# Split steps moved among gates in the mixer and among rotations, divisions and query copies in the attention of a two-block fp32 network

## What is computed

```python
def short_conv_mixer(h, w_in, conv_w, w_out):
    bcx = h @ w_in
    b_gate, c_gate, u = jnp.split(bcx, 3, axis=-1)
    y = b_gate * causal_depthwise_conv3(c_gate * u, conv_w)
    return y @ w_out

def swiglu(h, w_gate_up, w_down):
    g, u = jnp.split(h @ w_gate_up, 2, axis=-1)
    return (jax.nn.silu(g) * u) @ w_down
...
            kv = rmsnorm(h, kv_norm) @ w_kv
            k_sh = partial_rotary(k_sh.reshape(bsz, s, N_KV_HEADS, HEAD_DIM), cos, sin)
            q = (rmsnorm(h, b_pre_norm[j]) @ b_w_q[j]).reshape(bsz, s, N_HEADS, HEAD_DIM)
            q = partial_rotary(q, cos, sin)
            attn = sliding_window_sink_attention(q, k_sh, v_sh, b_sinks[j]) @ b_w_o[j]
            h = h + rmsnorm(attn, b_post_norm[j])
        ff = swiglu(rmsnorm(h, ffn_pre_norm[l]), ffn_w_gate_up[l], ffn_w_down[l])
```

## Time and profile before

| | |
|---|---|
| median of three runs | 1064.49 us (1064.3 to 1064.68) |
| profiled execution, its own time | 1063.95 us |
| its span, first to last instruction | 1062.1 us |
| TensorE busy | 1049.4 us, 99% |
| VectorE busy | 659.7 us, 62% |
| ScalarE busy | 567.0 us, 53% |
| GpSimd busy | 80.9 us, 8% |
| DMA, mean | 177 GB/s |
| granted TensorE clock, mean | 0.999 |

### The profile page before, as it was taken

How to read it: one execution, slowest core, us unless ns; L and a number is a source line. 1 busy time by engine, 2 the same in 40 slices (tenths; PEclk the granted TensorE clock), 3 DMA queues, 4 the chain that set the end, 5 groups by cost and what they waited for, 6 DMA issues and landing times.

```text
span 1062.1 us, 14789 instructions
## 1 busy us (share of the span) xinstructions
PE 1049.4 (99%) x5023; PEld 861.0 (81%) x5023; DVE 659.7 (62%) x956; ACT 567.0 (53%) x917; POOL 80.9 (8%) x170
## 2 busy tenths in 40 slices
PE   9999999999999999999999999999999999999997
PEld 6998888888877788888888888888887688888886
DVE  5867754546687875554667455456777675555544
ACT  5755644545677664444555444454566744443542
POOL 0034000000023040000001000000101110000001
PEclk9999999999999999999999999999999999999999
DMA  8573656556553354645565465656552253646541
GB/s 341 189 240 124 216 168 211 172 183 201 194 193 105 120 187 163 221 159 200 191 203 180 159 216 162 215 177 212 185 159 80 97 181 120 216 161 216 165 152 40
DMA packets 51883, 187.80 MB, mean 177 GB/s; under 512 B 5808, under 2 KB 5952, under 8 KB 51840
## 3 DMA queue, kind: packets, MB, share of 16 engines
q1 hardware_dynamic: 50688, 183.79, 51.6%
q0 software_dynamic: 864, 3.07, 1.0%
q10 hardware_dynamic: 288, 0.37, 0.1%
HBM read 186.15 MB, written 1.05 MB: 176 GB/s over the span
## 4 chain that ended last, share of the span: by engine, by line
PE 93%; DVE 4%; ACT 2%; issue 1%; POOL 0%; POOLq 0%; DVEq 0%; ACTq 0%
PE pG L1655 17%; PE pG L1653 17%; PE pG L1654 17%; PE pD L1653 11%; PE pD L1655 11%; PE pD L1654 11%; PE pT L1658 3%; DVE w_low L1323 2%; PE pG L1675 1%; PE pG L1658 1%; PE pG L1911 1%; PE pT L1796 1%; ACT w_high L1041 0%; PE pD L1658 0%; PE pD L1930 0%
## 5 line engine op out<-in xcount | busy, mean ns | idle before, releaser
L1323 DVE TENSOR_TENSOR w_low<-raw,w_high 128x1024 fp32r<-128x1024 f32 x340 | 411.2, 1225 | 118.6 <-ACT w_high L1041 104.7
L1041 ACT ACTIVATE w_high<-raw 128x1024 fp32r<-128x1024 f32 x340 | 353.2, 1055 | 79.1 <-PE pG L1655 65.7
L1653 PE MATMUL pG<-w_high,xTh 128*128 128x512 f32 (+1 forms) x816 | 319.8, 392 | 0.1
L1655 PE MATMUL pG<-w_high,xTl 128*128 128x512 f32 (+1 forms) x816 | 312.4, 383 | 0.0
L1654 PE MATMUL pG<-w_low,xTh 128*128 128x512 f32 (+1 forms) x816 | 312.1, 382 | 0.0
L1655 PEld LDWEIGHTS pG<-w_high,xTl 128*128 128x128 f32 x816 | 153.2, 188 | 27.9
L1654 PEld LDWEIGHTS pG<-w_low,xTh 128*128 128x128 f32 x816 | 153.6, 188 | 25.6
L1653 PEld LDWEIGHTS pG<-w_high,xTh 128*128 128x128 f32 x816 | 153.3, 188 | 25.6 <-DVE xTl L1356 0.3
L1653 PE MATMUL pD<-w_high,aTh 128*128 128x512 f32 x384 | 150.8, 393 | 0.0
L1655 PE MATMUL pD<-w_high,aTl 128*128 128x512 f32 x384 | 149.9, 390 | 0.0
L1654 PE MATMUL pD<-w_low,aTh 128*128 128x512 f32 x384 | 149.4, 389 | 0.0
(11 more groups left out here) (266 smaller groups left out, 808.6 us busy)
## 6 DMA issues: line engine op xcount, KB each, us to landing
raw<-in_stream SPq DMA_DIRECT2D x340, 512.0 KB, 4.4
post<-in_posts POOLq DMA_DIRECT2D x5, 512.0 KB, 4.7
early<-in_stream SPq DMA_DIRECT2D x4, 512.0 KB, 12.5
first_w<-in_stream SPq DMA_DIRECT2D x3, 512.0 KB, 6.0
h<-in_x SPq DMA_DIRECT2D x2, 512.0 KB, 5.5
out<-hg SPq DMA_DIRECT2D x3, 256.0 KB, 2.2
consts<-in_consts POOLq DMA_DIRECT2D x1, 417.0 KB, 4.2
out<-hg ACTq DMA_DIRECT2D x1, 256.0 KB, 2.7
```

The costliest lines, as they stand in the source:

```text
L1041: sc.activation(w_high[:, slot(static):slot(static) + CHUNK], raw_of(static), ACT.Copy).then_inc(w_high_done, 1)
L1323: ve.tensor_tensor(w_low[:, slot(static):slot(static) + CHUNK], raw_of(static), w_high[:, slot(static):slot(static) + CHUNK].bitcast(F32), ...
L1653: pe.matmul(dst, ah, hi, start=start, stop=False)
L1655: return pe.matmul(dst, al, hi, start=False, stop=stop)
```

## The change

No operation is added or removed; TensorE, GpSimd and SP have the same instructions in the same order. The change moves splits (and once a rotation) on ScalarE and VectorE:

- start of the mixer: the split of chunk 2 goes ahead of `T(0, 0)`;
- the split of chunk 13 goes from in front of `G(0, 3)` to behind it;
- in `walk_follower`, for blocks 2 to 6 of the mixer, `G(1, b)` goes ahead of the one split that stood in front of it, so that with the two splits that followed it three now stand in a row behind the gate (two for block 6);
- attention: `second(1)` goes ahead of `rope(0, 0)`; one split goes from behind `S(1)` to behind `N(1)`; the two splits around `QKT(0, 1)` go behind `proj(2, 1, 3)` and behind `S(3)`.

```diff
@@ walk_block_step
     if ph.mixer and s == 1:
         step("G", 1, 0, shift)
+    if ph.mixer and s == 3:
+        refill(step, freed, 1)
@@ walk_second_follower
-    refill(step, freed, 2)
+    refill(step, freed, 1)
@@ walk_follower
-    step("R", g, early, shift)
-    step("G", 1, b, shift)
+    if ph.mixer:
+        step("G", 1, b, shift)
+        step("R", g, early, shift)
+    else:
+        step("R", g, early, shift)
+        step("G", 1, b, shift)
@@ walk_attention
+    step("second", 1)
     step("rope", 0, 0)
     projects(0, 1, range(3))
-    step("second", 1)
...
     step("S", 1)
-    refill(step, freed, 1)
     step("E", 1)
...
     step("N", 1)
+    refill(step, freed, 1)
...
     step("N", 2)
-    refill(step, freed, 1)
     step("QKT", 0, 1)
     project(2, 1, 3)
+    refill(step, freed, 1)
     step("rope", 1, 1)
-    refill(step, freed, 1)
     step("PT", 2, 0)
     step("PT", 2, 1)
     step("S", 3)
+    refill(step, freed, 1)
@@ walk
     step("fill", 1, 1)
+    step("fill", 2, 1)
     step("T", 0, 0, 0, ph=MIX)
     step("first", 1, KT // 2, KT)
-    step("fill", 2, 1)
```

## The result

The changed kernel takes 1067.09 us (median of 11 runs, 1066.27 to 1069.32), the kernel before beside it 1064.72 us (11 runs, 1064.05 to 1065.82). The ratio is 1.0025, with a 95% interval of 1.0017 to 1.0032. So the change costs 2.4 us by the medians and 2.7 by the ratio, just beyond the 0.2% (2.1 us) that the prediction took as the border to slower; the interval reaches to both sides of that border. Forecast were +2.0 us and 1066.5. The median lies inside the stated range of 1064.9 to 1067.7, and 0.1 us above the 1067.0 up to which the prediction's own sum was to hold.

What follows compares the result with a forecast made beforehand. TensorE, busy 99% of the span, was taken as the bound, so only its pauses could change. Mixer -0.5 + 2.3 + 1.1 = +2.9, attention -0.95, sum +2.0 us on 1064.49: 1066.5 us, range 1064.9 to 1067.7.

Steps and rivals of the forecast that it cites:

- the prediction's own sum: Whole kernel: mixer +2.9 and attention -0.95 make +2.0 us, 1066.5 us; own range 1065.9 to 1067.0, chance 0.45.
- The removed pauses: Mixer, `T(0, 3)` and `T(1, 2)`: waits vanish, gaining 0.69 and 0.35 us, with 0.05 per transpose pair, together 1.1.
- `T(0, 4)`: Mixer: part of the gain given back through chunk 18's load, leaving 0.5 us gained for all up to here.
- `T(0, 5)`, `T(0, 6)`, `T(0, 7)`: Mixer: new waits for `act` of 0.60, 0.67 and 0.90 us, with 0.05 each, together 2.3 us lost.
- The working by margins: `T(0, 5)` to `T(0, 7)`: each pause is 1.14 us added, less idle time and the margin from `act` to `T`.
- End of the mixer: Block 6: two splits behind the gate delay the taps and TensorE turning `h` by 1.14 us, at least 1.0.
- Attention: -0.95 us: 0.45 at `proj(1, 1, 0)`, 0.5 at `PT(1)`, 0 at `S(3)` because the wait moves to `PV(2)`.
- (a): Rival, mixer: new splits stay hidden, its 1.1 and attention's 0.95 gains kept, no loss at its end; 1062.4 us, chance 0.10.
- (c): Rival, attention: `S(3)` pays after all because `prT` moves up, 0.86 us less, 1065.6 us; chance 0.10.
- (b): Rival, mixer: GpSimd makes splits dearer, last two pauses and mixer end lose 0.2 to 0.3 more each; 1067.2 us, chance 0.35.
- the case that had a chance of 0.43: Verdict on the whole kernel: slower than before by over 0.2% (2.1 us), border 1066.6 us.
- the case beside it: Verdict on the whole kernel: same, within 0.2% (2.1 us) of the kernel before; chance 0.51.

Runs made afterwards that it cites:

- short loads: Changed kernel with the loads of chunks 16 to 19 cut to half their bytes, so part computes on stale weights; one execution, 1066.05 us.
- the split put back: Changed kernel with only the split of chunk 13 back in its old place next to that of chunk 12; 1066.62 us, ratio 1.0023.
- the mixer part alone: Kernel before plus the change's mixer moves and the split ahead of `T(0, 0)`, attention as before; 1068.04 us, ratio 1.0036.
- the kernel with the swap in one follower: Changed kernel, but the gate goes ahead of the split only for follower block 2, not blocks 3 to 6; 1064.14 us, ratio 0.9996.
- the attention part with the split ahead of `E(2)`: Kernel before plus the change's attention moves, with the split behind `project(2, 1, 3)` moved ahead of `E(2)`; 1063.14 us, ratio 0.9985.
- the two attention kernels: Kernel before plus the attention part alone, 1062.79 us (ratio 0.9986), and the same with a split moved ahead of `E(2)`, 1063.14 us (0.9985).
- the kernel that moved the split of block 6: Kernel before, mixer splits two behind gate and two behind leader's `T`, block 6's split behind `D(1, 6)`, attention moves, one split ahead of `E(2)`; 1063.12 us, ratio 0.9988.

## Why the prediction came out as it did

**The removed pauses** were 0.77 and 0.42 us, forecast 1.1 together: right, by the distance between starts and not by the brackets of 0.53 and 0.19.

**`T(0, 4)` is the step that failed.** The prediction says: "The load and everything behind it come 0.5 us earlier, not 1.1." The issue of that load, of chunk 18, did come 0.6 us earlier, but the load landed 0.3 us later, and the splits, `act` and `T(0, 4)` came 0.3 us later with it. The forecast followed this one load, because the row in the trace of before names the wait for it, and took its time to landing as fixed; it was 4.4 us instead of 3.5. What was missed is the load in front of it. SP waits for the moved split of chunk 13 before it issues the load of chunk 17: 43.39 instead of 42.35. The prediction used the moved split to time the split of chunk 14, and did not ask for the load that hangs on it directly. It lands at 48.34, when ScalarE has been idle for 0.62 us, and until then the load of chunk 18 is under way beside it.

The row of four splits was missed at this block too. It costs its 0.6 us at `T(0, 4)` as at every later block, loads or not, and the prediction priced it only from `T(0, 5)` on. This did not show in the number by luck: booked was a pause of 0.6 by way of the load, and the row alone makes as much (+0.61 with short loads and with the split put back). The pause was 1.57, which is 1.0 us more. Smaller differences at the start, at `T(0, 3)` and in attention took 0.2 back.

**`T(0, 5)`, `T(0, 6)`, `T(0, 7)`**: forecast 0.65, 0.72 and 0.95, measured 0.66, 0.74 and 0.92. The working by margins, 1.14 us added less the 0.3 from the end of `act` to `T` and the idle time, holds to 0.1 us, and that the three add up is shown too. Taking the swap back in these followers removed all three.

**End of the mixer**: 1.14 forecast, 1.13 measured, and gone with the swap.

**Attention**: -0.95 forecast, -1.0 in the trace of the change. The wait moved from `S(3)` to `PV(2)`, with `prT` as its releaser, as written; taking the split out from in front of `prT` removed it.

**The rivals.** (a), the splits stay hidden, is refuted by four brackets. (c), `S(3)` pays, is refuted by the bracket of 0.73 at `PV(2)`. (b) would have given 1067.2, nearly the measured time, but it is not what happened: its mechanism was to make `T(0, 6)`, `T(0, 7)` and the end of the mixer dearer, and these came out at 0.74, 0.92 and 1.13, against 0.72, 0.95 and 1.14. GpSimd does stretch the splits. Timeline of VectorE and GpSimd at that place:

```profile
85.51 3.67 DVE L1329 TENSOR_TENSOR w_low<-raw,w_high 128x1024 fp32r<-128x1024 f32 x3 [0.60 <-ACT w_high L1047]
...
84.74 0.32 POOL L912 TENSOR_TENSOR trig<-trig 128x64 f32<-128x64 f32 x1
...
85.61 1.32 POOL L912 TENSOR_TENSOR trig<-trig 128x64 f32<-128x64 f32 x1
```

Three splits take 3.67 instead of 3.50 us, while GpSimd's operation takes 1.32 instead of 0.32: GpSimd pays, VectorE hardly. That fits the lock of the Trainium skill, SBUF — State Buffer, section "SBUF: two separate sides", with the splits mostly first and GpSimd second. A total near one case's number is no evidence for that case; its own places have to be looked at.

**The numbers.** 1066.5 was the base of three runs plus 2.0. Against more runs beside it the base was 0.2 us higher, and the change 0.4 (by the medians) to 0.7 us (by the ratio) dearer. The ratio of 1.0025 lies in the case that had a chance of 0.43, over the border of 0.2% that lay 0.1 us above the value; its interval (1.0017 to 1.0032) leaves the case beside it open.

## What to carry to other kernels

When a step moves in an engine's queue, list every load that the issuing queue releases behind it, and follow each to its first reader; the wait that the old trace shows is only the one that was last then. Do not carry a load's time to landing over when the load in front of it moves. An engine at 62% has no room in general but in places: count what stands between two points where the bounding engine needs it (here the follower's `act` and the leader's next `act`), and move work to where it is idle, since moving it behind one urgent operation puts it in front of the next. And price such a row at every block in which it stands, the first one too.

## What the hardware showed that was not expected

**Landing times.** How long a load of 512 KB takes to land goes with how much of the load in front of it is still to come. In the trace of before, the 87 loads (from chunk 16 on) that SP issued when the one in front had landed or had less than 1 us to go landed after 3.3 us in the median. The 169 that were issued when it had 2 us or more to go took 4.6 us. In the changed kernel these medians are 3.3 and 4.6 too. This is worked out from every issue and landing in the two traces; that the transfers share the queue's rate is the likely reason, which no run isolates. There is a scatter on top. Issued at the same point of the list and the same time, 46.20, that of chunk 18 landed at 51.14 in the mixer part alone and at 50.61 in the kernel with the swap in one follower. `T(0, 4)` paused there by 2.12 and 1.58 us: half a microsecond by nothing in the program. It may be why the changed kernel spreads over 3.0 us and the kernel before over 1.8; that was not tested. A rival is the granted clock: of the three longest runs of the changed kernel (1068.31, 1068.48 and 1069.32) the last two list 0.997 where the others have 0.998 or 0.999.

**The first microseconds.** The warming matmuls at the start run 0.43 us apart (512 columns, so 1.2 GHz) and then 0.21, and the point of the change differs by execution: up to 5.6 us in the execution of before, until 4.0 in that of the attention part with the split ahead of `E(2)`. The column of the granted clock says 1.00 in all of it, but it tells nothing there: the trace's records of the clock begin only where the pace rises, at 5.50 us before and at 3.82 in that kernel of attention, and the column counts a stretch without a record as 1.00. Where the low pace lasts longest, the first eight transposes are slow as well and everything behind them starts 0.6 us later. Timeline of TensorE, before:

```profile
2.87 2.98 PE L1664 MATMUL pD<-warm 128*128 128x512 bf16 x7
```

and in that kernel of attention:

```profile
3.29 1.73 PE L1664 MATMUL pD<-warm 128*128 128x512 bf16 x6
```

This is 1.2 us between the earliest and the latest execution, more than most of what was at stake here, and no part of any kernel's merit: the two attention kernels have the start of the kernel before, word for word, and begin 0.6 us earlier and 0.5 us later than it. The Trainium skill, TensorE: Matmul & The Clock Gate, section "Part 1: The HAM clock gate (the "warmup" mystery)", calls the number of slow matmuls at a start variable from run to run; these traces agree.

**A drift without pauses.** In two traces TensorE falls behind the trace of before with no single step above 0.03 us: by 0.3 us between 122 and 310 us with the split of chunk 13 put back, and by 0.35 us there and another 0.8 us behind 345 us in the kernel that moved the split of block 6. The others drift by less than 0.1 us in each of these stretches. The column of the granted clock reads 1.00 for all of them; the cause is open. A span alone, even between two profiled executions, is therefore not good to better than about 1 us, while the steps are.
